# Where the weight tensors begin in SBUF, against the activations they are multiplied with: a two-layer decoder trunk on one NeuronCore

## What is computed

```python
for l in range(2):
    h = rms_norm(x, attn_norm[l])
    proj = h @ w_in[l]                       # 1024 -> 3104 columns, for three mixers
    mix = concat(gated_delta_net(proj), sparse_attention(proj), short_conv(proj))
    x = x + mix @ w_out[l]                   # 1024 x 1024
    h2 = rms_norm(x, ffn_norm[l])
    gate, up = split(h2 @ w_gate_up[l])      # 1024 -> 2 x 2816
    x = x + (silu(gate) * up) @ w_down[l]    # 2816 -> 1024
```

## Time and profile before

| | us |
|---|---|
| median of three runs | 1334.44 |
| the profiled execution | 1334.45 |
| its span, first to last instruction | 1332.7 |
| TensorE busy | 1323.6 |
| VectorE busy | 740.5 |
| GpSimd busy | 650.7 |
| ScalarE busy | 625.5 |

### The profile page before, as it was taken

One profiled execution on the slowest core, in us unless ns is written; L12 is line 12 of the kernel. 1 busy time (PEld: TensorE's weight loads), 2 busy tenths in 40 slices (PEclk: granted clock), 3 DMA queues, 4 the chain that ended last, 5 costly groups with the idle time before them and its releaser, 6 DMA issues.

```text
span 1332.7 us, 22375 instructions
## 1 busy us (share of the span) xinstructions
PE 1323.6 (99%) x8936; PEld 1165.9 (87%) x8936; DVE 740.5 (56%) x1450; ACT 625.5 (47%) x1223; POOL 650.7 (49%) x454
## 2 busy tenths in 40 slices
PE   8999999999999999999999999999999999999999
PEld 7888887778899889998879888887889998899987
DVE  5637777723876137771165387777248751477611
ACT  5563436636556225552335543467355542356511
POOL 4458307644454544554343663176425554354552
PEclk9999999999999999999999999999999999999999
DMA  6415300114334224333222362001233333334322
GB/s 168 129 38 161 95 17 1 33 48 88 95 96 123 92 90 115 106 96 119 88 85 78 74 168 68 1 5 30 64 95 95 96 96 110 95 96 121 101 88 86
DMA packets 176583, 114.91 MB, mean 86 GB/s; under 512 B 48224, under 2 KB 154976, under 8 KB 176480
## 3 DMA queue, kind: packets, MB, share of 16 engines
q1 hardware_dynamic: 174368, 113.22, 29.9%
q10 hardware_dynamic: 2112, 0.26, 0.1%
HBM read 109.80 MB, written 3.67 MB: 85 GB/s over the span
## 4 chain that ended last, share of the span: by engine, by line
PE 94%; DVE 2%; POOL 1%; ACT 1%; issue 1%; DMA 1%; SPq 0%; DVEq 0%; ACTq 0%
PE ps L796 35%; PE ps L1277 29%; PE ps L1178 7%; PE ps L846 6%; PE ps L935 2%; PE ps L1083 2%; PE ps L1122 2%; PE ps L1105 2%; PE ps L1092 1%; PE ps L861 1%; PE ps L1131 1%; POOL arena L1913 1%; PE ps L915 1%; PE ps L1044 1%; PE ps L737 1%
## 5 line engine op out<-in xcount | busy, mean ns | idle before, releaser
L1816 POOL TENSOR_TENSOR w_lo<-w_raw,w_hi 128x2048 fp32r<-128x2048 f32 (+2 forms) x59 | 264.4, 4481 | 312.9 <-ACT w_hi L1382 245.0
L1382 ACT ACTIVATE w_hi<-w_raw 128x2048 fp32r<-128x2048 f32 (+2 forms) x61 | 113.9, 1867 | 232.9 <-PE ps L796 161.6
L1834 POOL TENSOR_TENSOR aT_lo<-ffn_tmp,aT_hi 128x512 fp32r<-128x512 f32 x44 | 63.6, 1445 | 167.3 <-ACT aT_hi L1429 167.3
L2562 DVE SCALAR_TENSOR_TENSOR x_tok<-ps,st,x_tok 128x512 f32<-128x512 f32 x32 | 23.8, 749 | 144.2 <-PE ps L796 144.2
L796 PE MATMUL ps<-w_hi,aT_hi 128*128 128x512 f32 x352 | 95.8, 390 | 0.0
L796 PE MATMUL ps<-w_lo,aT_hi 128*128 128x512 f32 x352 | 95.4, 389 | 0.0
L796 PE MATMUL ps<-w_hi,aT_lo 128*128 128x512 f32 x352 | 95.4, 389 | 0.0
L1390 ACT ACTIVATE w_hi<-w_raw 128x512 fp32r<-128x512 f32 x38 | 24.0, 632 | 131.9 <-PE ps L1277 96.0
L796 PE MATMUL ps<-hT_hi,w_lo 128*128 128x512 f32 x320 | 81.0, 393 | 0.0
L796 PEld LDWEIGHTS ps<-w_lo,aT_hi 128*128 128x128 f32 x352 | 66.1, 188 | 13.8
L796 PEld LDWEIGHTS ps<-w_hi,aT_lo 128*128 128x128 f32 x352 | 66.1, 188 | 13.8
(11 more groups left out here) (383 smaller groups left out, 3339.0 us busy)
## 6 DMA issues: line engine op xcount, KB each, us to landing
w_raw<-in_w_gate_up SPq DMA_DIRECT2D x88, 512.0 KB, 5.1
w_raw<-in_w_in SPq DMA_DIRECT2D x21, 1024.0 KB, 5.4
w_raw<-in_w_down SPq DMA_DIRECT2D x16, 1024.0 KB, 5.0
w_raw<-in_w_down SPq DMA_DIRECT2D x8, 768.0 KB, 4.5
w_raw<-in_w_out SPq DMA_DIRECT2D x16, 256.0 KB, 4.0
w_raw<-in_w_out SPq DMA_DIRECT2D x8, 512.0 KB, 5.0
w_raw<-in_w_in SPq DMA_DIRECT2D x2, 1056.0 KB, 7.1
x_tok<-in_x SPq DMA_DIRECT2D x4, 512.0 KB, 4.9
```

Of the source, the lines that this page charges most:

```text
L1382: nc.scalar.activation(whi[:, c % 2, 0:kt * w], raw[:, c % 2, 0:kt * w], ACT.Copy).then_inc(S["w_hi"], 1)
L1816: nc.gpsimd.tensor_tensor(wlo[:, c % 2, 0:kt * w], raw[:, c % 2, 0:kt * w], whi[:, c % 2, 0:kt * w].bitcast(F32), ALU.subtract).then_inc(S ...
L1834: nc.gpsimd.tensor_tensor(alo[:, cnt % FT, :], ft[:, cnt % 2, :], ahi[:, cnt % FT, :].bitcast(F32), ALU.subtract).then_inc(S["a_lo"], 1)
```

## The change: 32 bytes in front of the weights

It inserts a tensor of SKEW = 8 floats (32 bytes) in front of w_raw, moves five small tensors (st, gsc, peb, glc, att; with the old 40-byte spacer, rounded to 64, they are 2048 bytes) from in front of x_tok to behind w_lo, adds EVEN = 8 floats behind them, and inserts 32 bytes in front of t_ring. No instruction is added, removed or moved.

```diff
 N_SLOTS = 24
+SKEW, EVEN = 8, 8
...
-        st = sb("st", [P, 9, 32])
         gbuf = sb("gbuf", [P, NT, 8])
-        gsc = sb("gsc", [P, 9, NT * GH])
         ngt = sb("ngt", [P, NT, 3 * NH])
-        peb = sb("peb", [P, 2])
...
         state = sb("state", [P, 2, P])
-        glc = sb("glc", [P, NT, 2])
-        att = sb("att", [P, 2, 24])
-        sb("spacer", [P, 10])
         x = sb("x_tok", [P, NT, D])
...
         hlo = sb("hT_lo", [P, KD, T], F32R)
+        sb("skew", [P, SKEW])
         raw = sb("w_raw", [P, 2, KD * SLOT])
...
         whi, wlo = sb("w_hi", [P, 2, KD * SLOT], F32R), sb("w_lo", [P, 2, KD * SLOT], F32R)
+        st = sb("st", [P, 9, 32])
+        gsc = sb("gsc", [P, 9, NT * GH])
+        peb = sb("peb", [P, 2])
+        glc = sb("glc", [P, NT, 2])
+        att = sb("att", [P, 2, 24])
+        sb("even", [P, EVEN])
         rbt = sb("rbt", [P, T])
...
         slo = ffn.enter_context(nc.sbuf_tensor("sT_lo", [P, KD, T], F32R))
+        ffn.enter_context(nc.sbuf_tensor("ffn_skew", [P, SKEW], F32))
         t_ring = ffn.enter_context(nc.sbuf_tensor("t_ring", [P, N_TSLOTS - 1, 2, T], F32R))
```

## The result

The changed kernel takes 1344.7 us in the median (1344.53 to 1344.89, five runs) against 1334.66: a ratio of 1.0076, interval 1.0065 to 1.0087. It is 10 us slower where 8.9 us of gain were forecast. Nothing was added and nothing waits longer, so the whole difference is pitch. What they are read by is the length of the gate-up pieces and of the first down piece of the chain, which agree between the two layers within 0.02 us in every run.

What follows compares the result with a forecast made beforehand. TensorE, busy 1323.6 of 1332.7 us, was taken as the bound, so matmul pitch decides. Gains of 4.4 us (256 columns) and 4.5 us (wider products) made 1334.4 - 8.9 = 1325.5 us, range 1320 to 1334.6 (0.85).

Steps and rivals of the forecast that it cites:

- What bounds the kernel: TensorE, busy 1323.6 of 1332.7 us at full clock; only a matmul's pitch or a new stall can move the time.
- Unit price: Gain per matmul from the 32-byte skew, read from t_last against t_ring: 1.5 ns, readings allowing 1.3 to 1.8.
- term 1: 256-column gate-up products (L1277) not yet skewed, weight stationary: 2,928 x 1.5 ns = 4.4 us of gain.
- Term 2: 512-column products and 192 of 288 columns, weight stationary or moving: 2,976 x 1.5 ns = 4.5 us of gain.
- Rival D: Slower: skew keeps 512-column products from settling fully, some 231 ns, costing 11.7 us; 1341.7 us, chance 0.08.
- Rival B: Only products with the weight stationary gain, with the weight moving nil: 5.8 us off, 1328.6 us; chance 0.13.
- Rival C: Nothing happens: t_last's figures come from that slot's place, not its 32 bytes; 1334.4 us, chance 0.10.
- the rule of two ports: Skill's rule that TensorE reads moving operand and weights through independent ports, so address distance costs nothing and time stays.
- terms 3 to 5: Attention matmuls over idle_w (0.4 us either way, uncounted), other engines, and loads into w_raw with 5.7 us room: nothing.
- The last sentence of the prediction: Warned that t_last was skewed among aligned neighbours, whereas after the change other weights are skewed too; no size given.

Runs made afterwards that it cites:

- run at 80 and 64 bytes: Against the kernel before: fast-block weights moved 80 bytes, t_ring and t_last at 64, other chunks except zg 192; 1337.29 us.

## Why the prediction was wrong

**What bounds the kernel:** right. TensorE's list and its pitch decide, and no wait entered.

**Unit price and term 1, the narrow products:** right. 1.5 ns were read from t_last, 2,928 x 1.5 = 4.4 us expected, 4.7 measured in the pieces, and the run that keeps only this half gained 1334.9 - 1329.9 = 5.0 us. The weight loads fell from 190 to 188 ns as said.

**Term 2, the wide products:** this is the step that failed: 4.5 us of gain (2,976 x 1.5 ns) were counted where 14.8 us of loss came. The text bounded the effect from below by "no gain" and took 1.5 ns "because the excess to be cut is the same 13.3 to 13.5 ns at all three widths". The trace held no wide product with a skew, so the lower bound should have reached below nothing: the measured value is 5.3 ns the other way over the 2,784 wide products, 14.8 us by the run with them alone, and nothing for the 192 of 288 columns. An equal excess at distance 0 says nothing of the change of it with distance. Nor do the weight loads, by which the lower bound was reasoned: in the down products they went from 188 to 187 ns while the pitch rose by 6.6. The sum should have been 4.4 us of gain from the narrow and an open term of either sign on 2,784 matmuls, where 1.6 ns decide.

**Rival D** named that point and the place (a wide pitch of 231 ns), and had a chance of 0.08. Its price of 4.2 ns was near the 5.3 measured. Its mechanism, a sequence kept from its settled pitch, is not what the runs show: with the skew the wide settle too, on a higher pitch (233.3 ns as the mean of all 264 down products). It was priced low because it was taken for a disturbance.

**Rival B, that only a stationary weight counts:** wrong. The plain blocks, weight stationary, lost 6.5 ns, the down products, weight moving, 6.6. That the two sit on opposite sides of their partners does matter, though not at 32 bytes: see the table at 8, 16, 64 and 192.

**Rival C, and the rule of two ports:** a common shift of 32 bytes left the gate-up and down pieces within 0.01 us, the same shift of one side alone changed both widths. So the two reads of TensorE do influence each other through their distance, against what the Trainium skill ("TensorE: Matmul & The Clock Gate", Step-by-step: what each phase is for) leads one to expect of independent ports. The gap that the Trainium skill gives for an isolated matmul on the same page (Back-to-back issue gap: N / 2.4 + 2.5 ns) makes 109 and 216 ns, an estimate; no stretch here reached it, the lowest pitches are 113.4 and 226.7.

**The small tensors, the other engines and the loads (terms 3 to 5):** right as nothing. The common shift has w_raw at 160 and takes the time of before, and the two halves of the change add up to the whole without the move of the small tensors.

**The last sentence of the prediction** doubted that t_last, skewed among aligned neighbours, stands for a whole stretch. At 32 bytes it did, 118.5 against 118.4 ns. At 64 bytes no such row could have stood for it: the same products run at 113.6 or 117.9 ns by what goes ahead.

What stays open is the mechanism. The runs show a dependence on the distance down to 8 bytes, aligned again at 256, a gain for 256 and a loss for 512 moving columns, and a memory at 64 bytes. None of them shows why gain turns to loss with the width, what a stretch keeps from its entry, or how that goes with the run at 80 and 64 bytes, where nothing ahead of the first stretch was moved by 64 and the t_ring products still ran at 114.3 ns. That a semaphore wait or another engine's access sets the state was not tried.

## What to carry to other kernels

Where TensorE is the bound, the distance modulo 256 bytes between stationary and moving fp32r operands, with its sign, is a parameter to be tried for each width of matmul by itself, and a neighbour's value must not be carried over to another width: give a part of the kernel without an example in the trace both signs. Shift data inside a slot rather than the tensor, so that each kind of product has its own distance. After that, read the pitch stretch by stretch; if it differs between stretches of like products, alter the chunk ahead of the slower one.

## What the runs showed of the hardware

- A matmul's pitch depends on the distance between its operands' addresses: 113.6 to 120.0 ns for 256 columns and 226.7 to 234.3 for 512 at the same granted clock, the 2.4 GHz level. 0 and 256 bytes are alike.
- For 512 columns the sign counts: with the weight moved by 64 bytes 233.3 ns where it is stationary and 228.9 where it is moving, by 192 bytes 229.1 and 233.3.
- With one distance a matmul can have two pitches. With the weight moved by 64 bytes, a stretch of 672 or 924 matmuls of 256 columns runs throughout at 113.6 or throughout at 117.9 ns. A lead of 36 moved matmuls was worth 4.0 us behind it in one place, and one of 48 nothing in another.
- A common offset of 32 bytes for all large tensors is worth nothing: 1334.6 against 1334.9 us.
